# A decoder block in four batches of two chunks, in place of one, two, three and two

## The reference, cut to what matters

```
h = rmsnorm(x, mix_norm_g);  q, k, v, gb, gc, hc = split(h @ w_in, 6)
o_attn[t] = sum over s < t of sigmoid(z_ts) * prod_{s<j<t}(1 - sigmoid(z_tj)) * v[s]
o_conv = gb * causal_conv3(gc * hc)
x = x + concat(rmsnorm(o_attn), rmsnorm(o_conv)) @ w_out
xn = rmsnorm(x)
# for each token and each of 8 heads: top 16 of 128x128 experts by two lists of 128 keys
s1, s2 = (xn @ wq) . keys[0], (xn @ wq) . keys[1]
best, pos = top16(top16(s1)[:, None] + top16(s2)[None, :]);  g = softmax(best)
x = x + sum_k g_k * gelu(xn . u_tab[idx_k]) * v_tab[idx_k]
out = rmsnorm(x)
```

## Time and profile before

| | us |
|---|---|
| median of three runs | 3229.57 |
| lowest and highest | 3228.86, 3231.71 |
| the profiled execution | 3231.53 |
| its span, first to last instruction | 3229.7 |
| VectorE busy | 2484.3 (77%) |
| TensorE busy | 2381.8 (74%) |
| DMA moved | 1212.80 MB, mean 376 GB/s |

### The profile page before, as it was taken

One profiled execution on the slowest core, in us unless ns is written; L12 is line 12 of the kernel. 1 busy time (PEld: TensorE's weight loads), 2 busy tenths in 40 slices (PEclk: granted clock), 3 DMA queues, 4 the chain that ended last, 5 costly groups with the idle time before them and its releaser, 6 DMA issues.

```text
span 3229.7 us, 28947 instructions
## 1 busy us (share of the span) xinstructions
PE 2381.8 (74%) x7374; PEld 1257.9 (39%) x7374; DVE 2484.3 (77%) x5530; ACT 998.4 (31%) x2280; POOL 1522.3 (47%) x1488
## 2 busy tenths in 40 slices
PE   8669886679889697676887888777677755555655
PEld 7537454246545253222554434344333311111111
DVE  1666779867898689887677888869977778887887
ACT  2131521331565311234115756412122221112111
POOL 0132323333443343555544545544455567775775
PEclk9879988889898898898997999988899877776777
DMA  6879699899888999999999999999999999999998
GB/s 235 314 304 362 253 370 367 339 367 400 347 345 317 358 389 354 359 390 354 419 419 397 380 377 413 392 420 415 382 402 413 421 401 422 422 422 399 422 422 336
DMA packets 185036, 1212.80 MB, mean 376 GB/s; under 512 B 20673, under 2 KB 20673, under 8 KB 53441
## 3 DMA queue, kind: packets, MB, share of 16 engines
q0 software_dynamic: 147456, 1073.81, 82.3%
q1 hardware_dynamic: 37440, 137.40, 11.1%
HBM read 1198.54 MB, written 12.58 MB: 375 GB/s over the span
## 4 chain that ended last, share of the span: by engine, by line
DVE 32%; PE 26%; DMA 23%; ACT 11%; issue 6%; POOL 1%; SPq 0%; DVEq 0%; POOLq 0%; ACTq 0%
DMA ring<-in_uv,cur_idx 21%; DVE ring L1136 14%; PE vacc L961 8%; DVE acc L1156 7%; PE bank L999 7%; PE bank L1067 3%; ACT L757 3%; PE bank L995 2%; ACT g_ge L778 2%; PE bank L1078 1%; DMA xn<-in_final_norm_g 1%; PE o_ps L965 1%; ACT diag L782 1%; DVE lt L1273 1%; DVE ocT L1283 1%
## 5 line engine op out<-in xcount | busy, mean ns | idle before, releaser
L961 PE MATMUL vacc<-ring,diag 128*128 128x512 f32 x1886 | 1179.9, 752 | 763.1 <-ACT diag L782 759.1
L739 POOL DMA_INDIRECT ring<-in_uv,cur_idx x1024 | 1203.9, 1176 | 1035.2 <-PE vacc L961 473.2
L1136 DVE CUSTOM_DVE_ANT_0 ring<-ring,xn 128x1024 f32<-128x1024 f32 x1024 | 1228.1, 1220 | 242.0 <-DMA ring<-in_uv,cur_idx 238.8
L961 PEld LDWEIGHTS vacc<-ring,diag 128*128 128x128 f32 x1886 | 395.6, 227 | 1413.0 <-ACT diag L782 1059.3
L1156 DVE SCALAR_TENSOR_TENSOR acc<-ring,g_w,acc 128x512 f32<-128x512 f32 (+1 forms) x840 | 674.4, 803 | 40.0 <-DVE g_w L1145 0.3
L730 POOL COPY cur_idx<-idx 128x2 uint32<-128x2 uint32 (+2 forms) x448 | 316.4, 706 | 645.4 <-DVE acc L1156 495.7
L778 ACT ACTIVATE g_ge<-dots 128x2 f32<-128x2 f32 (+1 forms) x448 | 91.3, 204 | 1688.8 <-DVE dots L1136 1688.3
L782 ACT ACTIVATE diag<-ident,g_w 128x128 f32<-128x128 f32 x943 | 324.1, 393 | 125.3 <-DVE g_w L1145 124.2
L999 PE MATMUL bank<-hT,wpool 128*128 128x256 f32 (+2 forms) x1280 | 287.9, 384 | 1.4 <-ACT hT L809 1.4
L999 PEld LDWEIGHTS bank<-hT,wpool 128*128 128x128 f32 x1280 | 222.0, 194 | 75.2 <-issue 18.5
L757 ACT ACT_TABLE_LOAD x187 | 239.9, 1283 | 4.1 <-PEq L1421 0.8
(11 more groups left out here) (129 smaller groups left out, 1603.7 us busy)
## 6 DMA issues: line engine op xcount, KB each, us to landing
wpool<-in_w_in SPq DMA_DIRECT2D x96, 512.0 KB
wpool<-in_peer_wq SPq DMA_DIRECT2D x64, 512.0 KB
wpool<-in_w_out SPq DMA_DIRECT2D x32, 512.0 KB
ring<-in_uv,cur_idx POOLq DMA_INDIRECT x1024
xb<-in_x SPq DMA_DIRECT2D x15, 512.0 KB
x_scratch<-xb SPq DMA_DIRECT2D x8, 512.0 KB
xn_scratch<-xb SPq DMA_DIRECT2D x8, 512.0 KB
xn<-xn_scratch SPq DMA_DIRECT2D x8, 512.0 KB, 7.8
```

The source lines that it names most:

```text
L739: nc.gpsimd.indirect_dma_start(ring[:, s, :], None, uv, bass.IndirectOffsetOnAxis(ap=cur_idx[:, s:s + 1], axis=0))\
L961: ins = nc.tensor.matmul(vacc[:, :], diag[:, q * group_of(c) + s, :], ring[:, q * group_of(c) + s, D:D + PE_COLS], start=first and s == 0, ...
L1136: ins = nc.vector.tensor_tensor_reduce(out=ring[:, s, 0:D], in0=ring[:, s, 0:D], in1=xn[:, c % 2, :], scale=1.0, scalar=0.0, op0=ALU.mult, ...
```

## The change

BATCHES becomes four pairs. Batch 0 now has chunks 0 and 1, so their norm, projection (256 moving columns in place of 128), attention, mix and queries all stand ahead of chunk 0's first gather. Chunk 0's searches come where they did, among the queries; chunk 1's four searches of two heads follow behind the queries, one part of a group of chunk 0 with each step. Batches 1, 2 and 3 then run beside chunks 0-1, 2-3 and 4-5. TMAX falls from 384 to 256. The x of chunk 1 is loaded at the start into `acc` number 0 and read there again at the mix, so it needs neither the wait for `xb` nor the second load. The condition in `narrow_groups` changes from "not larger than the batch before" to "smaller", so it is now true for no batch and all three give narrow groups. The `load_chunk` of chunks 0 and 1 waits for both spills, and that of chunk 1 for the last search of batch 0.

```diff
-BATCHES = [[0], [1, 2], [3, 4, 5], [6, 7]]
+BATCHES = [[0, 1], [2, 3], [4, 5], [6, 7]]
...
-        if c > chunks[0]:
+        if c > chunks[0] and bi > 0:
             at(d, "sp", "load_x_again", c)
...
-    if bi > 0:
-        k += 4
-        for c in chunks:
+    k += 8 if bi == 0 else 4
+    if len(chunks) > 1:
+        for c in chunks[1 if bi == 0 else 0:]:
             for h in range(0, PH, hs):
                 search(at, k, c, h)
...
-        if len(BATCHES[b]) <= len(BATCHES[b - 1]):
+        if len(BATCHES[b]) < len(BATCHES[b - 1]):
             continue
         found |= {ph[1:3] for ph in line[first:last] if ph[0] == "group" and ph[3] == 0}
...
+        x_home = lambda c: acc[:, 0, :] if c == 1 else xb[:, 0, :]
...
-            if c == 0:
+            if batch_of(c) == 0:
                 return xn[:, 1, :], acc[:, 1, :]
...
+                    if c == 1:
+                        sp.dma_start(x_home(c), x[0, c * P:(c + 1) * P, :]).then_inc(s_x1, 16)
+                        return
...
-                        sp.wait_ge(s_exp, found(0, PH - 1))
-                    sp.wait_ge(s_spx, 32 * (c + 1))
+                        sp.wait_ge(s_exp, found(BATCHES[0][-1], PH - 1))
+                    sp.wait_ge(s_spx, 32 * (max(c, BATCHES[0][-1]) + 1))
...
-                    ss(nc.scalar.activation(xb[:, 1, :], xb[:, 0, :], ACT.Square, accum_out=st[:, 0:1]))
+                    ss(nc.scalar.activation(xb[:, 1, :], x_home(c), ACT.Square, accum_out=st[:, 0:1]))
...
-                                                             scalar=st[:, 6 + part:7 + part], in1=xb[:, 0, cols],
+                                                             scalar=st[:, 6 + part:7 + part], in1=xb[:, 0, cols] if part else x_home(c)[:, cols],
```

More of the change, by code:

```diff
@@ L223, in timeline @@
                     out.append(("front", "sp", "load_chunk", 0))
-                known = (args[1] + heads_per_search(0)) * TOPK // group_of(0)
+                if args[0] == 0:
+                    known = (args[1] + heads_per_search(0)) * TOPK // group_of(0)
     steps = {bi: front_steps(bi) for bi in range(1, len(BATCHES))}
@@ L370, in build @@
     n_tiles = per_batch * len(BATCHES)
-    loads = [(name, *args) for _, name, *args in phases if name in ("load_x", "load_x_again")]
+    loads = [(name, *args) for _, name, *args in phases if name in ("load_x", "load_x_again") and args != [1]]
     x_loads = {what: i + 1 for i, what in enumerate(loads)}
@@ L492, in build @@
         s_x = sem("s_x")
+        s_x1 = sem("s_x1")
         s_ss = sem("s_ss")
@@ L678, in _ @@
                         front(name, args)
+                        front("load_x", [1])
                         while state["w"] < WSLOTS:
@@ L682, in _ @@
                         sp.dma_start(keys_home, keys).then_inc(s_keyload, 16)
-                    else:
+                    elif name != "load_x" or args[0] != 1:
                         front(name, args)
@@ L793, in front @@
                         act.wait_ge(s_const, 16)
-                    act.wait_ge(s_x, 16 * x_loads[("load_x", c)])
+                    if c == 1:
+                        act.wait_ge(s_x1, 16)
+                    else:
+                        act.wait_ge(s_x, 16 * x_loads[("load_x", c)])
                     if c - 1 in BATCHES[bi]:
                         act.wait_ge(s_full, use_no[("turn_h", c - 1, 1)] + 1)
-                    ss(nc.scalar.activation(xb[:, 1, :], xb[:, 0, :], ACT.Square, accum_out=st[:, 0:1]))
+                    ss(nc.scalar.activation(xb[:, 1, :], x_home(c), ACT.Square, accum_out=st[:, 0:1]))
                     ss(nc.scalar.activation(st[:, 1:2], st[:, 0:1], ACT.Ln, bias=eps[:, 0:1], scale=1.0 / D))
                     ss(nc.scalar.activation(st[:, 2:3], st[:, 1:2], ACT.Exp, scale=-0.5))
-                    nc.scalar.activation(xb[:, 1, :], xb[:, 0, :], ACT.Copy, scale=st[:, 2:3]).then_inc(s_hn, 1)
+                    nc.scalar.activation(xb[:, 1, :], x_home(c), ACT.Copy, scale=st[:, 2:3]).then_inc(s_hn, 1)
                 elif name == "store_h":
                     c, = args
-                    if c > 0:
+                    if batch_of(c) > 0:
                         act.wait_ge(s_exp, found(BATCHES[batch_of(c)][0] - 1, PH - 1))
@@ L1240, in front @@
                         dve.wait_ge(s_act_free, freed_by[("sum", c)][1])
-                        if c > 0:
+                        if ("load_x_again", c) in x_loads:
                             dve.wait_ge(s_x, 16 * x_loads[("load_x_again", c)])
```

## The result

| | before | after |
|---|---|---|
| median of four runs, us | 3230.64 | 3306.99 |
| lowest and highest | 3228.86, 3232.51 | 3304.92, 3313.07 |
| ratio, 95% interval | | 1.0236 (1.0223 to 1.025) |
| profiled execution, its span | 3231.5, 3229.7 | 3313.07, 3311.3 |

The kernel became 2.4% slower, 76 us by the medians and 81.6 us by the spans. The forecast was 3335 us. The sign and the order of size were right, and the time lies in the range. The profiled execution of the kernel after was the slowest of its four, 6 us above their median, so a working from its trace has to come out at 81.6 us and not at 76.

What follows compares the result with a forecast made beforehand. DMA engines set a floor of 2.55 us a row, plus each stage's surplus beyond it. Longer start and searches +154, refund -83 and VectorE's adds +35 made +106 us: 3335 us, range 3250 to 3395.

Steps and rivals of the forecast that it cites:

- Norm, turn, store: Start, ahead of projection: chunk 1 passes the same three engines after chunk 0's store, +6.4 us.
- Projection: Batch 0's projection: 256 moving columns take 17.27 us where 128 take 8.93; with the v tiles, +40.5 us.
- Attention and mix: First score to first query: a full second mix, four partly hidden blocks and the spill, +42 us.
- Query to first product: End of the start: lists at double width every 3.9 us and a longer search stretch, +21 us.
- Searches beside the first rows: First product to batch 1's projection: 6.5 searches and six double lists remain on VectorE, +42 to +44 us.
- The refund: Batches 1 to 3: front work spread over about 250 rows each lowers their surplus, -83 us.
- VectorE adds more: Narrow groups in equal batches: 171 wide adds in place of 81, half hidden under DMA, +35 us.
- (1) Full refund: Later batches: all run at DMA's pace like batch 3, VectorE's additions hidden, 3246 us; chance 0.12.
- (2) Faster: Full refund, and searches after the first product hide too as gathers fill the queues, 3202 us; chance 0.07.
- (3) Hardly any refund: Later batches: they keep batch 2's prices, refund only -11 us, 3408 us; chance 0.11.
- (4) Width free: Batch 0's projection on TensorE: columns don't set the pace, 33.4 us don't come, 3302 us; chance 0.02.
- (5) No move: Whole order: the change doesn't move the work; chance 0.02 together with any other.

Runs made afterwards that it cites:

- early tokens: Changed kernel with load_chunk of chunk 0 issued right behind chunk 1's spill, ahead of the weights: 3297.70 us, ratio 1.0195.
- the emptied search: Changed kernel with top_pairs and look_up of chunk 1 returning at once, so its searches are left out: 3287.60 us, ratio 1.0167.
- the batches of 1, 2, 2, 3: Kernel before with BATCHES set to [[0], [1, 2], [3, 4], [5, 6, 7]]: 3278.01 us, ratio 1.0127.
- the late norm: Changed kernel with norm_x of batches 1 to 3 placed some two groups behind its load_x: 3312.03 us, ratio 1.0232.
- the halves: Changed kernel with batch 0's projection (all kinds but v) done 128 moving columns at a time: 3310.52 us, ratio 1.0238.

## Why the prediction was right, point by point

**What bounds the kernel.** The floor of 2.55 us a row held: the last two chunks run at 324 us for 128 rows, at DMA share 0.98. The working by surplus could be repeated on the kernel after.

**Norm, turn, store** +6.4: measured 17.74 - 11.41 = +6.3. **Projection** +40.5: 86.2 against 45.5, +40.6. **Attention and mix** +42: 79.9 against 38.4, +41.5. The first two rest on durations of the same steps in the trace of before, counted, and nothing else runs there. The third had a second mix of 25.2 us, which took 26.5 (157.36 to 183.81), and 17 us for four blocks and the spill, a judgement between 2 and 27 that came out at 15. That it was so near is in part luck. The +9 us that the working gives for the projection if width were nearly free doesn't come out of its own figures (with the v tiles they make 11 to 14), but nothing else in the sum rests on it.

**Query to first product** +21: measured 67.1 against 39.7, +27. The lists do come every 3.9 us (196.31, 200.21), as forecast. The step that failed is one that the working didn't have: the queue that `load_chunk` stands in. Before, the gathers were last, ends on a wait for one. After, the slots of `wpool` come free later (the query tiles leave every 3.9 us in place of 2.0), and the tokens land last. With early tokens the first product is 13.4 us earlier. The stretch is then +14 and not +21, so the terms that the working did have were 7 us too dear: the first gather goes out 17 us later behind the first query than before (46 us for 29), and the first row is there 7.6 us after it in place of 10.4. The miss of 6 us is the difference of these two.

**Searches beside the first rows**, +42 to +44: measured +20. VectorE had 141.35 us of work there, as against the 144 counted. The step that failed is the division by 0.835. That share came from a stretch in which VectorE also waited for gathers; in the longer one the gathers waited for VectorE, as a DMA share of 0.66 says, and it was 117.46/122.0 = 0.96 busy until the last search. The mechanism is right: the emptied search gave back 17 to 22 us.

**The refund**, -83: measured -64. By batch 95, 109 and 133 us were 114, 116 and 126. For whole batches the estimate by front per row was of the right size (the batches of 1, 2, 2, 3 follow it as well) and the refund came out a quarter smaller. Inside a batch it doesn't hold. Attention parts 37, 51 and 75 us were 38, 63 and 55: beyond the 20 us for weights and x a block costs 1.3, 1.9 and 1.2 us at 0.24, 0.30 and 0.35 blocks a row, so it isn't dearest where the blocks are densest, and the sum of 155 against 163 is two errors that cancel. The rest of the batches, 58 each, was 76, 54 and 71, 27 us in all too little, with 78, 86 and 80 rows beside each chunk.

**VectorE adds more**, +35: the counts are exact (171 wide adds at 1285 ns, 72 us more busy) and no price can be seen: without the narrow groups the ratio is lower by 4 us, with 8 us of noise. The step that failed took half of an engine's added work as path. VectorE at 0.87 busy, the highest share of a part, could be taken to 0.80 with nothing gained, though TensorE took the work over there.

**What wasn't in the sum**: the handovers, +14. The load of x took 12.3 and 9.8 us in them, and 11.1 in one of before's, so it isn't what is new. What makes the rest stays open; as the late norm shows, taking the wait away doesn't give the time back.

In the sum +106 stood against +84 by the same account: -23 (searches), -35 (adds), +19 (refund), +6 (tokens) and +14 (handovers) make -19 of the -22, and the rest is rounding and the last chunks' -1. Two terms that were too dear outweighed three that were too cheap. The sign and the main terms were reasoned; that misses of 97 us, added without their signs, left 22 is luck.

**The rivals.** (1) Full refund, 3246: no. Batches had surpluses of 114 to 126 and not 94. (2) Faster, 3202: its condition came about by half. VectorE did pass 0.9, but the DMA share beside it was 0.66, so the rows were held up. (3) Hardly any refund: no. (4) Width free: no, by the halves. (5) No move: no.

**What would show it.** The first product (250.9) is in 235 to 255, chunks 2-3 and 4-5 take 788 and 793 us of the 770 to 800, the last chunks 324 of 326. Batch 1's projection starts at 405.5 and not near 415: the first product was 6 us late, and the stretch behind it 154.6 us with 42 rows in place of 172 with 40.

## What to carry to other kernels

Here work ahead of the first gather cost about its full time, so in a kernel that DMA bounds look for a small first batch; what the later batches got back was less, since only their part above the floor can be saved. A share of busy time read from a stretch in which the engine also waited is no ceiling for it: ask what it waited for there, and whether that wait is still there after the change. Follow each queue past the point that moves: the one DMA behind the weights cost more (10 to 13 us) than all the work of turning a second chunk (6.3). And don't count a wait as a gain before a run has shown that its time isn't given back later.

## What the runs showed of the hardware

The same 0.5 MB load takes very different times: 3.8 us at the start of the program, 12.4 behind eight weight tiles, the gain and the keys, 15.1 for the tokens among the first eight gathers (the later of two loads together), and 12.3 in the handover. VectorE can be 0.96 busy over 122 us beside DMA at 0.66. A float32 product's time follows its columns from 128 to 256 at a ratio of 1.93, and cutting it in two costs 3% (17.87 us against 17.27). An activation table load is 1.28 us long with no gap of more than 0.03 us ahead of it in the stretches looked at, and 200 of them fewer, 257 us of ScalarE, made the kernel 37 us faster.
